# Feed-forward layers as one block each, the router inside the norm, and a mixture's gather spread over its experts

## What is computed

```python
# first block, twice (layer 0 on 512 + 256 tokens, layer 1 on 512)
h = h + g2 * conv_ffn(modulate(rmsnorm(h, norm2_g), sh2, sc2), w_up, w_dw, b_dw, w_down)

def conv_ffn(h, w_up, w_dw, b_dw, w_down):
    u = dwconv(h @ w_up, w_dw, b_dw)        # w_up: 1024 x 5632, 3 taps along the tokens
    a, b = jnp.split(u, 2, axis=-1)
    return (jax.nn.silu(a) * b) @ w_down    # w_down: 2816 x 1024

# second block: mixer, memory attention, then
x = x + expert_choice_moe(rms_norm(x, g_ffn), w_router, w_gate, w_up, w_down)
return rms_norm(x, g_final)

def expert_choice_moe(h, w_router, w_gate, w_up, w_down):     # 16 experts
    cap = 2 * 512 // 16                                        # 64 tokens per expert
    aff = softmax(h @ w_router)
    gates, idx = top_k(aff.T, cap)
    xin = h[idx]                                               # 16 x 64 x 1024
    y = (silu(xin @ w_gate) * (xin @ w_up)) @ w_down           # three 1024 x 1024 per expert
    return zeros.at[idx].add(y * gates)
```

## Time and profile before

| | us |
|---|---|
| median of 3 runs | 2844.97 |
| lowest and highest | 2839.74, 2846.42 |
| profiled execution, whole | 2844.73 |
| profiled execution, first to last instruction (span) | 2842.8 |
| PE busy | 2483.6 (87%) |
| DVE busy | 1185.7 (42%) |
| ACT busy | 853.7 (30%) |
| mean granted PE clock, as a share of 2.4 GHz | 0.931 |
| read from HBM | 380.22 MB |

### The profile page before, as it was taken

One profiled execution on the slowest core, in us unless ns is written; L12 is line 12 of the kernel. 1 busy time (PEld: TensorE's weight loads), 2 busy tenths in 40 slices (PEclk: granted clock), 3 DMA queues, 4 the chain that ended last, 5 costly groups with the idle time before them and its releaser, 6 DMA issues. The chain is left out here.

```text
span 2842.8 us, 35098 instructions
## 1 busy us (share of the span) xinstructions
PE 2483.6 (87%) x14248; PEld 1764.7 (62%) x14248; DVE 1185.7 (42%) x1718; ACT 853.7 (30%) x1293; POOL 29.8 (1%) x57
## 2 busy tenths in 40 slices
PE   5988789989998989898989987988797779998997
PEld 3872477878887866576777875765686553222222
DVE  2688325542355132573562543554423331222223
ACT  3210334321233041473441432454434321000001
POOL 0000000000000001000000000000000000000000
PEclk7998799999999989899899998999899889999998
DMA  5138211111111125002222222110131309999996
GB/s 216 60 98 297 114 60 45 66 69 51 52 59 63 64 101 234 18 1 75 67 94 84 93 97 80 51 48 23 61 118 37 133 9 401 422 421 421 421 422 256
DMA packets 74741, 390.87 MB, mean 137 GB/s; under 512 B 9072, under 2 KB 12400, under 8 KB 43760
## 3 DMA queue, kind: packets, MB, share of 16 engines
q1 hardware_dynamic: 74608, 388.97, 36.2%
HBM read 380.22 MB, written 2.10 MB: 134 GB/s over the span
## 5 line engine op out<-in xcount | busy, mean ns | idle before, releaser
L258 DVE TENSOR_TENSOR WLO<-RAW,WHI 128x1024 fp32r<-128x1024 f32 (+3 forms) x226 | 279.1, 1235 | 837.1 <-ACT WHI L247 837.1
L274 PE MATMUL PS<-XNH,WHI 128*128 128x512 f32 (+1 forms) x1856 | 583.3, 359 | 43.3 <-DVE WLO L258 15.7
L274 PE MATMUL PS<-XNH,WLO 128*128 128x512 f32 (+1 forms) x1856 | 577.6, 356 | 0.0
L274 PE MATMUL PS<-XNL,WHI 128*128 128x512 f32 (+1 forms) x1856 | 577.2, 356 | 0.0
L247 ACT ACTIVATE WHI<-RAW 128x1024 fp32r<-128x1024 f32 (+3 forms) x226 | 241.4, 1068 | 1009.7 <-PE PS L274 983.1
L274 PEld LDWEIGHTS PS<-XNH,WHI 128*128 128x128 f32 x1856 | 317.3, 191 | 103.4 <-DVE WLO L258 25.8
L274 PEld LDWEIGHTS PS<-XNL,WHI 128*128 128x128 f32 x1856 | 317.5, 191 | 51.6 <-issue 1.0
L274 PEld LDWEIGHTS PS<-XNH,WLO 128*128 128x128 f32 x1856 | 316.2, 190 | 51.1
L2307 PE MATMUL PS<-RAWM,XS 128*64 128x512 f32 x1024 | 245.6, 603 | 40.4 <-DMA RAWM<-experts 38.8
L274 PE MATMUL PS<-HH,WHI 128*128 128x512 f32 (+1 forms) x528 | 163.0, 363 | 32.9 <-PEq L905 32.9
L2307 PEld LDWEIGHTS PS<-RAWM,XS 128*64 128x64 f32 x1024 | 64.9, 136 | 198.1 <-DMA RAWM<-experts 107.2
(11 more groups left out here) (299 smaller groups left out, 2676.8 us busy)
## 6 DMA issues: line engine op xcount, KB each, us to landing
RAWM<-experts SPq DMA_DIRECT2D x192, 1024.0 KB, 27.0
ADAW<-ada SPq DMA_DIRECT2D x48, 1024.0 KB, 8.2
RAW<-up SPq DMA_DIRECT2D x88, 512.0 KB, 3.3
RAW<-down SPq DMA_DIRECT2D x32, 704.0 KB, 4.1
RAW<-pw SPq DMA_DIRECT2D x24, 512.0 KB, 3.5
V<-V SPq DMA_DIRECT2D x64, 101.0 KB, 2.7
RAW<-qkv SPq DMA_DIRECT2D x12, 512.0 KB, 3.5
RAW<-w_in SPq DMA_DIRECT2D x10, 512.0 KB, 3.5
```

Source lines behind the costliest of these rows:

```text
L258: dve.tensor_tensor(prog.WLO[:, at % SPLITS, 0:to.length], prog.RAW[:, at % RAWS, 0:to.length], f32(prog.WHI[:, at % SPLITS, 0:to.length]) ...
L274: last = pe.matmul(prog.PS[:, to, a:b], w, x[:, k, a:b], start=(k == 0 and n == 0), stop=(k == g.k - 1 and n == 2))
```

## The change

Feed-forward: `ffn_up` and its `project` calls become one function `conv_ffn` that runs up, down, up, down in one block for all engines. Its down projections start with `multiply_first`, whose third argument is now a function that waits for one chunk.

```diff
-def multiply_all(prog, pe, g, xh, xl, segments, psum_free, before, wait=lambda i, s: None):
+def multiply_all(prog, pe, g, xh, xl, segments, psum_free, ready, wait=lambda i, s: None, before=0):
...
-        pe.wait_ge(before.lo, k + 1)
+        ready(k)
...
+def chunks_of(pe, norm):
+
+    return norm and (lambda k: pe.wait_ge(norm.lo, k + 1))
...
+def conv_ffn(prog, ups, downs, layer, segments, gate, before):
...
+            norm.on_scalar(act)
+            prog.use_table_of(act, ACT.Silu)
+            for grp in range(2):
+                run_units(act, ups[grp].n, lambda i, s: up(grp, i, s))
+                run_units(act, downs[grp].n, lambda i, s: split_hi_ahead(prog, act, downs[grp], i, s))
...
+            for grp in range(2):
+                multiply_all(prog, pe, ups[grp], prog.XNH, prog.XNL, lambda u: segments, psum_free,
+                             None if grp else chunks_of(pe, norm), before=first(grp, False))
+                multiply_all(prog, pe, downs[grp], HH, HL, lambda u: segments, psum_free,
+                             lambda k: pe.wait_ge(hid_lo[grp], 2 + k + 1), before=first(grp, True))
```

```diff
+            if early:
+                sp.dma_start(moe.R[:], prog.dram["router"]).then_inc(r_landed, 16)
+                sp.dma_start(moe.IOTA[:], prog.dram["iota"]).then_inc(r_landed, 16)
             run_units(sp, g.n, lambda i, s: load_ahead(prog, sp, g, i, s))
...
+            if early:
+                act.wait_ge(r_landed, 32)
+                act.activation(moe.RH[:], moe.R[:], ACT.Copy).then_inc(r_hi, 1)
             run_units(act, g.n, step)
...
-            pe.wait_ge(r_lo, 1)
+            norm.on_tensor(pe)
 
             for k in range(KD):
-                for n, (x, w) in enumerate(((prog.XNH, RH), (prog.XNH, RL), (prog.XNL, RH), (prog.XNL, RL))):
+                pe.wait_ge(norm.lo, k + 1)
+                for n, (x, w) in enumerate(((prog.XNH, moe.RH), (prog.XNH, moe.RL), (prog.XNL, moe.RH), (prog.XNL, moe.RL))):
...
+            norm.on_scalar(act)
+            prog.use_table_of(act, ACT.Exp)
...
+            act.activation(WORK[E, :], PS[E, 1, 0:LAT], ACT.Copy).then_inc(rows_kept, 1)
             act.activation(moe.GATE_HI[E, :], PS[E, 1, 0:LAT], ACT.Copy).then_inc(gate_hi, 1)
-            act.activation(ROW[E, 1, :], PS[E, 1, 0:LAT], ACT.Copy).then_inc(rows_kept, 1)
+            act.activation(PROBS[E, :], PS[E, 1, 0:LAT], ACT.Copy).then_inc(gate_hi, 1)
...
-            dve.tensor_tensor(moe.GATE_LO[E, :], ROW[E, 1, :], f32(moe.GATE_HI[E, :]), ALU.subtract)
-            then(dve.tensor_copy(WORK[E, :], ROW[E, 1, :]))
...
+            dve.tensor_tensor(ROW[E, :], RANK[E, :], SEL[E, :], ALU.mult).then_inc(slots, 1)
             dve.tensor_tensor(moe.RANKS[E, :], RANK[E, :], SEL[E, :], ALU.mult)
+            dve.wait_ge(gate_hi, 2)
+            dve.tensor_tensor(moe.GATE_LO[E, :], PROBS[E, :], f32(moe.GATE_HI[E, :]), ALU.subtract)
```

```diff
-RING = 13
-EARLY = 7
+EARLY, LATE = 8, 6
+LATE_FROM = 138
 UNIT = 2 * D
+GROUP, GROUPS = 4, EXPERTS // 4
+def gather_spots():
+    return {(GROUP * (grp - 1) + 3 * k // KD, 3 * k % KD): (grp, k) for grp in range(1, GROUPS) for k in range(KD)}
+def ring_slots(units):
...
+        if g < LATE_FROM:
+            slot = g % EARLY
+        elif g < LATE_FROM + LATE:
+            slot = EARLY + g - LATE_FROM
+        else:
+            slot = min(last, key=last.get)
...
+        self.whole = [t[:] for t in early] + [prog.X[:, :, LAT:TOK]] + [t[:] for t in late]
...
+            for g in range(EARLY, UNITS):
+                if moe.before[g] is not None:
+
+                    sp.wait_ge(done, moe.before[g] + 1)
+                elif g == LATE_FROM:
+
+                    sp.wait_ge(gathered, GROUPS * KD)
                 load_unit(prog, sp, g)
```

```diff
+            def gather(grp, k):
+
+                if k < 2:
+                    pe.wait_ge(one_hot, NT * (grp + 1))
+                if KD * grp + k >= 2:
+                    pe.wait_ge(rows_kept[k % 2], (KD * grp + k) // 2)
+                for t in range(NT):
+                    for n, src in enumerate((moe.HTH, moe.HTL)):
+                        last = pe.matmul(G_PS[k % 2], src[:, t, k * P:(k + 1) * P],
+                                         moe.S[:, t, grp * GROUP * CAPACITY:(grp + 1) * GROUP * CAPACITY],
+                                         start=(t == 0 and n == 0), stop=(t == NT - 1 and n == 1))
+                last.then_inc(gathered, 1)
...
+            for k in range(KD):
+                gather(0, k)
+            rows_ready()
             for j in range(PART):
                 unit(first_gate(0) + j, j, lambda k: XS[:, 0, k, :], A_PS)
             for e in range(EXPERTS):
...
+                    gather_here(e, j)
...
+                        gather_here(e, PART + j)
...
+                rows_ready()
                 if e >= 1:
                     scatter(e - 1, 0)
...
+            mark(0)
+            for k in range(1, KD, 2):
+                keep_rows(0, k)
+            for grp in range(1, GROUPS):
+                mark(grp)
             for e in range(EXPERTS):
+                keep_here(e, range(PART + 1))
                 dve.wait_ge(b_turned, e + 1)
                 dve.wait_ge(silu, e + 1)
```

More of the change, by code:

```diff
@@ L861, in _ @@
                 load_unit(prog, sp, u)
+            if early:
+                sp.wait_ge(r_landed, 32)
         @block.scalar
@@ L976, in _ @@
+            dve.nop().then_inc(psum_free, 4)
+            for grp in range(2):
+                dve.nop().then_inc(hid_lo[grp], 2)
+            norm.on_vector(dve)
+            for grp in range(2):
+                run_units(dve, ups[grp].n, lambda i, s: up(grp, i, s))
+                run_units(dve, downs[grp].n, lambda i, s: down(grp, i, s))
         @block.tensor
         def _(pe):
-            if before is not None:
-                before.on_tensor(pe)
-            multiply_all(prog, pe, g, prog.XNH, prog.XNL, lambda u: segments, psum_free, before)
+            norm.on_tensor(pe)
@@ L2078, in __init__ @@
         self.GATE_LO = kept.take("GATELO", [P, LAT], F32R)
+        self.SLOT_T = kept.take("SLOTT", [P, LAT // P, EXPERTS])
+        self.IOTA = kept.take("IOTA", [P, CAPACITY])
         self.scratch = kept.at_
-        self.scratch_end = (prog.top - EARLY * UNIT * 4) // 64 * 64
-        self.RAW = [prog.at(f"RAWM{j}", [P, UNIT], F32, self.scratch_end + j * UNIT * 4) for j in range(EARLY)]
-        self.RAW += [prog.at(f"RAWM{EARLY + j}", [P, UNIT], F32, ring + j * UNIT * 4) for j in range(late)]
@@ L2085, in router @@
-def router(prog):
+        self.scratch_end = (prog.top - (EARLY - 1) * UNIT * 4) // 64 * 64
+        self.R = kept.take("R", [P, KD, P])
+        self.RH, self.RL = kept.take("RH", [P, KD, P], F32R), kept.take("RL", [P, KD, P], F32R)
+        self.unsplit = kept.at_
+        early = [prog.at(f"RAWM{j}", [P, UNIT], F32, self.scratch_end + j * UNIT * 4) for j in range(EARLY - 1)]
+        late = [prog.at(f"RAWM{EARLY + j}", [P, UNIT], F32, ring + j * UNIT * 4) for j in range(LATE)]
+        self.whole = [t[:] for t in early] + [prog.X[:, :, LAT:TOK]] + [t[:] for t in late]
@@ L2088, in router @@
+        self.half = [lambda c, t=t: t[:, c * 512:(c + 1) * 512] for t in early]
+        self.half += [lambda c: prog.X[:, 2 * c:2 * c + 2, LAT:TOK]]
+        self.half += [lambda c, t=t: t[:, c * 512:(c + 1) * 512] for t in late]
+        self.slots, self.before, self.use = ring_slots(UNITS)
+def router(prog, before):
     moe = prog.moe
     with prog.block("router") as block:
-        reg = prog.region(moe.scratch, moe.scratch_end)
+        norm = before(prog.region(prog.small_end + 3 * 24576, prog.moe.slots_at))
+        reg = prog.region(moe.unsplit, moe.scratch_end)
```

285 lines of the change are left out of this document (141 added, 144 removed).

## The result

| | before | after |
|---|---|---|
| median, us | 2842.72 (4 runs) | 2795.31 (4 runs, 2791.69 to 2807.91) |
| profiled execution, whole | 2844.73 | 2798.08 |
| span | 2842.8 | 2796.2 |
| mean granted PE clock | 0.931 | 0.938 |
| PE, DVE, ACT busy | 2483.6, 1185.7, 853.7 | 2484.9, 1188.6, 856.3 |

The ratio is 0.984, with a 95% interval of 0.9805 to 0.9876. A second set of five runs of the same kernel, beside other runs of the kernel before, gave 2798.41 and 0.9822 (0.9798 to 0.9846). The forecast was 2789, in a range of 2776 to 2806. In the spans, which the forecast's sum can be held against, 46.6 us went where 55.7 were forecast. The forecast's own terms say where the missing 9 us are. First the page of after, to be held against the earlier trace rows: its GB/s slices and the line of DMA packets.

The account below looks back on a forecast made before the run. TensorE was taken to pace 2347 us and the stream of 1 MB weight units the expert stage. Savings of 19.5 + 16.5 + 23.6 less 3.9 made 55.7 us, giving 2789 us, range 2776 to 2806.

Parts of the forecast that it names:

- Part 1: Feed-forward layers as one block each: less PE idle at block boundaries and some clock gain, 19.5 us saved.
- Part 2: Router matmuls inside the norm, following it chunk by chunk, and an earlier top-k start: 16.5 us saved.
- Part 3: Gather by groups: only the first group precedes the first expert matmul, the others hide behind the stream; 23.6 us saved.
- Rival (a): Expert stage: PE becomes the bound of experts 0 to 10, giving 2806 us; chance 0.08.
- Part 4: Ring of eight weight buffers, one in half of X with 1 KB rows: costs 3.9 us, bounds 0 and +10.
- Rival (b): Router, gather and feed-forward gaps: the clock falls and stays low, together 11 us, giving 2800; chance 0.10.
- Rival (c): Expert stream: small-row units delay it like transfers nothing overlaps, 58.5 us more, giving 2847, no change; chance 0.02.
- A: Experiments' theory for the expert stream: each unit written into X in 1 KB rows costs about 0.6 us, not 0.23.
- (d): Expert stage: the clock drops to 1.2 GHz, 19.8 us more per slow expert; four give 2868; chance 0.02.
- (e): Feed-forward up to down: the wait stays whole because ACT splits late, giving back 18 us, 2807; chance 0.04.

Follow-up runs that it names:

- the kernel that uses X once: Changed kernel with the half of X taking only unit 7, the ring then turning over seven whole-row buffers: 2785.56 us median, ratio 0.9788.
- the kernel with the spare buffer: Changed kernel with X taking only unit 7, plus an eighth whole-row buffer in spare room that takes unit 8: 2781.00 us median, ratio 0.9775.

## Why the prediction was right, and where it was off

**Part 1** (forecast 19.5). The gaps came out as written: 3.34 us for 3.25 at up to down, 2.15 and 2.5 us for the third unit, none at down to up. The two layers were shorter by 7.0 and 10.85 us, 17.8 together. That is not the true size of the part, and that it comes so near 19.5 is in part luck: the execution of before had the quicker of two paces in layer 0 (see the last section), 3.2 us in its first up stage alone, whose code is unchanged, and by an estimate some 8 to 9 us in the whole layer (11.3 us of gaps and 4.3 of clock went, and the layer was only 7.0 shorter). Against the profile of the four-block form, which had the slower pace too, it is 23.8 us, of which 18.1 are gaps (forecast 18.5) and 5.7 are clock (forecast 1, bounds -2 and 10). The medians give 16 to 19. So the gaps were right, and the clock part was taken too low.

**Part 2** (forecast 16.5). Measured 16.2 with the earlier compare, 17.35 forecast for both. Nearly all of the missing 1.1 us is that compare: the forecast let the first gather matmul wait for one compare, a quarter as long (+0.85), but `gather` waits for `NT * (grp + 1)` of them, all four of the first group. They take 1.43 us, and the matmul starts 1.49 behind their start, where it started 1.28 behind before: -0.2 instead of +0.85. The last router matmul was forecast for 2275.9 on the old time; its result is copied at 2257.04, which on the old time (19.0 later) is 2276.0.

**Part 3** (forecast 22.8 for the stretch, costs nothing behind the units). Measured 22.8, and 23 when it was undone. The cover of the spread chunks was real: doubling them cost nothing in the changed kernel. Rival (a) is out; with a stream of whole-row units the margin is some 1.7 us per expert on the average, where the forecast's numbers left 1.1 in an expert that gathers (5.0 - 3.3 - 0.6).

**Part 4** (forecast -3.9, measured -11.4). This is the step that failed: "+0.23 for each of 19 units". Its mechanism was right, rows of 1 KB slow the stream, and the list of 19 units was right. The size was taken from memT's 373 to 393 GB/s, a single transfer seen in eight slices of 0.25 us; within a full stream a unit in 1 KB rows takes 3.01 us and not 2.72. With 0.52 each, 19 units are 9.9 us. The upper bound of 0.5 us per unit was in the text, and it was nearly the truth; the part as a whole came out beyond its own upper bound of 10. The total stayed within its range because that range had room for rivals that did not come. The rest of the term was taken at -0.5 (eight preloaded units, stream starting behind the first unit); the kernel that uses X once shows 496.9 - 495.6 = +1.3. Together 11.2 of 11.4.

The Trainium skill, DMA: Bandwidth & Descriptors, Specifications, would have had these rows at line rate, since they are longer than 512 B. The trace disagrees: 348 GB/s with 1 KB rows, 381 with 2 KB (one unit in eight still at 1 KB), 421 with 8 KB. It was right to trust the row of the trace over the page, and wrong to take a price from a transfer that stood alone.

Rival (b), the clock, did not come: the router's matmuls ended as forecast and the gather took 10.44 us. Rival (c) is A carried to the extreme, and it was not that dear. Rivals (d) and (e) have no trace: in the changed kernel the clock is 1.00 from 2320 to 2740 us, and the gaps at up to down are 3.34 us.

## What to carry to other kernels

When a buffer is squeezed into a gap of another tile, look at the length of its rows and price them in a stream that is already full: a stream-bound stage pays for every row, and it pays in full. Work spread behind the units of such a stage is free only up to the margin of the engine that does it, and cutting it into smaller pieces can use that margin up; test it by doubling the work. Take the stage's own clock (here HT to HT) and the time from its first instruction to the end, since medians of the whole kernel also carry what the other stages did in that run.

## What the hardware showed unexpectedly

**Two paces of the same matmuls.** In the long up stages PE runs pairs of 512 and 256 columns without a gap at clock 1.00, yet some executions do 925 matmul records in 160 us and others 908. The windows of the changed kernel and of the one with the spare buffer:

```profile
460.00:620.00 160.00, 160.00 (x908) 1.00 0.20 68
```

```profile
460.00:620.00 160.00, 160.00 (x925) 1.00 0.21 71
```

That is 0.353 and 0.3465 us a pair. The code and the data are the same there in every kernel, and three of the thirteen profiled executions, the one before among them, had the quicker pace in this window. It is not a matter of the one-block form, and not of the whole execution either. From 700 to 900 us, most of it the second up stage, the kernel with the spare buffer had the slower pace, and the ones with 1 KB rows, 2 KB rows and the spare buffer with doubled chunks had changed to the quicker one; the changed kernel first, then the last of these:

```profile
700.00:900.00 200.00, 200.00 (x1133) 1.00 0.19 61
```

```profile
700.00:900.00 200.00, 200.00 (x1156) 1.00 0.19 65
```

With the clock behind the gaps this moved layer 0 between 574.6 and 587.1 us in the eleven executions with one block. Layer 1, with 512 columns alone, stayed within 384.3 and 387.1. Its cause is open.

**The same gap, another clock.** Behind the 3.34 us gap of layer 0 the granted clock stayed at 1.00 in the changed kernel, and fell to 1.2 GHz for the next six microseconds in the kernel with the spare buffer, whose code is the same up to there:

```profile
629.43:635.43 6.00, 6.00 (x34) 1.00 0.35 120
```

```profile
629.61:635.61 6.00, 6.00 (x19) 0.51 0.34 120
```

Gaps of 2.13 and 2.15 us had both outcomes as well (0.72 over the six microseconds behind the first one of the changed kernel, 1.00 behind the second). So the clock term of a gap of this size can only be given as a range.

**A matmul of 128 columns for the price of 256.** With float32 operands and a new 128 x 128 weight tile each time, both forms start 0.213 us apart at 1.2 GHz, and 0.112 and 0.12 us at 2.4 GHz.

**A price of some 9 ns for each further DMA packet of an engine** in a full stream, nearly equal at rows of 1, 2 and 4 KB.
